# FFN 2's down-projection for token chunks 0 and 1 by Strassen's seven products

## The reference

```python
def swiglu(x, w_in, w_out):
    gate, up = jnp.split(x @ w_in, 2, axis=-1)
    return (jax.nn.silu(gate) * up) @ w_out
...
    y = h + 0.5 * rmsnorm(swiglu(rmsnorm(h, p['ffn2_pre']), p['ffn2_w_in'], p['ffn2_w_out']), p['ffn2_post'])
```

## Time and profile before

| | |
|---|---|
| time, median of 3 runs | 3401.08 us (3397.26 to 3401.41) |
| span of the profiled execution | 3400.1 us, 70872 instructions |
| PE busy | 3305.8 us, 97% of the span |
| DVE busy | 1871.2 us, 55% |
| ACT busy | 1456.3 us, 43% |
| POOL busy | 700.0 us, 21% |
| granted TensorE clock, mean | 0.987 of full speed |
| DMA | 390.03 MB, mean 115 GB/s |

### The profile page before, as it was taken

One profiled execution on the slowest core, in us unless ns is written; L12 is line 12 of the kernel. 1 busy time (PEld: TensorE's weight loads), 2 busy tenths in 40 slices (PEclk: granted clock), 3 DMA queues, 4 the chain that ended last, 5 costly groups with the idle time before them and its releaser, 6 DMA issues. The chain is left out here.

```text
span 3400.1 us, 70872 instructions
## 1 busy us (share of the span) xinstructions
PE 3305.8 (97%) x28190; PEld 3137.6 (92%) x28190; DVE 1871.2 (55%) x3334; ACT 1456.3 (43%) x3056; POOL 700.0 (21%) x651
## 2 busy tenths in 40 slices
...
GB/s 167 76 79 79 87 109 230 221 135 81 70 70 70 71 70 70 109 254 369 188 47 56 58 59 59 59 59 136 165 88 70 123 86 76 76 76 151 200 207 132
DMA packets 353606, 390.03 MB, mean 115 GB/s; under 512 B 22792, under 2 KB 259416, under 8 KB 353134
## 3 DMA queue, kind: packets, MB, share of 16 engines
...
## 5 line engine op out<-in xcount | busy, mean ns | idle before, releaser
L673 PE MATMUL ps<-p_hi,w_hi 128*128 128x352 f32 x912 | 305.6, 335 | 1.8 <-PEq L123 1.4
L673 PE MATMUL ps<-p_hi,w_lo 128*128 128x352 f32 x912 | 294.5, 323 | 0.0
L673 PE MATMUL ps<-p_lo,w_hi 128*128 128x352 f32 x912 | 294.0, 322 | 0.0
L2062 PE MATMUL ps<-p_hi,w_hi 128*128 128x352 f32 x840 | 291.0, 346 | 2.7 <-PEq L123 1.4
L2062 PE MATMUL ps<-p_hi,w_lo 128*128 128x352 f32 x840 | 277.2, 330 | 0.0
L2062 PE MATMUL ps<-p_lo,w_hi 128*128 128x352 f32 x840 | 277.2, 330 | 0.0
L673 PEld LDWEIGHTS ps<-p_hi,w_hi 128*128 128x128 f32 x912 | 173.1, 190 | 4.2 <-issue 2.7
L2897 PE MATMUL ps<-op_hid_hi,w_hi 128*128 128x384 f32 (+1 forms) x528 | 171.5, 325 | 3.7 <-DVE w_lo L2572 2.0
L673 PEld LDWEIGHTS ps<-p_lo,w_hi 128*128 128x128 f32 x912 | 173.2, 190 | 0.0
L2897 PE MATMUL ps<-f_hid_hi,w_hi 128*128 128x352 f32 x528 | 171.5, 325 | 1.6 <-DVE w_lo L2572 1.6
L673 PEld LDWEIGHTS ps<-p_hi,w_lo 128*128 128x128 f32 x912 | 172.2, 189 | 0.0
...
## 6 DMA issues: line engine op xcount, KB each, us to landing
w_raw<-in_ffn_w_out_dram SPq DMA_DIRECT2D x136, 256.0 KB, 3.4
w_raw<-in_w_in_dram SPq DMA_DIRECT2D x67, 512.0 KB, 4.2
sa_v<-in_cache_v_dram SPq DMA_DIRECT2D x120, 256.0 KB, 6.7
w_raw<-in_ffn_w_in_dram SPq DMA_DIRECT2D x48, 512.0 KB, 5.1
sa_k<-in_cache_k_dram SPq DMA_DIRECT2D x72, 256.0 KB, 5.5
f_s<-in_ffn_w_out_dram SPq DMA_DIRECT2D x64, 256.0 KB, 3.5
pair_s<-in_ffn_w_out_dram SPq DMA_DIRECT2D x64, 256.0 KB, 3.2
d_hid<-f_gb SPq DMA_DIRECT2D x44, 264.0 KB, 2.1
```

The lines of the kernel that those rows point to most:

```text
L673: mm = nc.tensor.matmul(m.ps[:, bank, 0:CH], a[:, k, w], b[:, f, cols(c)], start=(f == 0 and i == 0), stop=(f == KT - 1 and i == 2))
L2062: mm = nc.tensor.matmul(m.ps[:, (k + c) % 2, 0:CH], a[:, k, f * P:(f + 1) * P], x[:, f, cols(c)], start=(j == 0), stop=(j == len(terms) - 1))
```

## The change

`ffn_units` gets an argument `quads`, which only FFN 2 passes. For chunks 0 and 1 (768 tokens) the product of 2816 x 1024 weights and 768 tokens is cut in halves along all three axes, and computed with seven products of half the size in each direction instead of eight. A product is now called a pass p (0 to 6); it has KH = 11 units, v = 11 p + k, each again with 4 x 3 matmuls of 384 columns. Chunk 2 keeps the direct product (units 77 to 120, `rest_step`).

- Weights: five passes need the sum or difference of two 128 x 512 tiles, in 55 units in all. SP loads both into the same ring of 8 raw slots (132 loads where there were 88), DVE adds them in place (`w_sum`), and only then ACT and DVE split the sum. Four of the raw slots are freed by `w_low`, the others by `w_sum`.
- Activations: POOL issues accumulating DMAs from DRAM to DRAM during the first half of FFN 2 (`add_stored`, `add_lower`: 11 each into `d_sum`, `d_first` and two parts of `d_hid`); SP stores each of the first 11 tiles twice more as their start (`store_sums`). One operand is made by DVE (`x_sum`, L2723 of the kernel after, 3 pieces). The operand of a pass is loaded whole, a pass ahead, and split in 3 pieces of 4, 4 and 3 tiles (`x_high`, `x_low`, 128 x 1536 or 128 x 1152) instead of 44 pieces of 128 x 384.
- Results: ACT and DVE add each pass's 4 banks to one or two of the four blocks of the output in SBUF during the next pass (`read_act`, `read_dve`), so squares, root, scaling, residual and transposes of chunks 0 and 1 get new places.
- Chunk 2's activations are split by ACT and POOL (`rest_high`, `rest_low`) during pass 6 and after it.

The core of the diff:

```diff
+    SOURCES = (((1, 1),), ((0, 1), (1, 1)), ((0, 0), (1, 0)), ((0, 0), (1, 1)), ((1, 0), (1, 1)), ((0, 0),), ((0, 1), (0, 0)))
...
+    def load_raw(sp, r):
+        v, n = RAWS[r]
...
+        elif RAWS[r - 8][1] == 1:
+            sp.wait_ge(e.w_sum, SUM_OF[RAWS[r - 8][0]])
+        else:
+            sp.wait_ge(e.out_lo, RAWS[r - 8][0] + 1)
...
+    def add_stored(pool, s):
...
+        pool.dma_start(d_first[j], hid_part(s, 0), accum_op=ALU.add).then_inc(e.added[0], 16)
+        pool.wait_ge(e.h_out[1], 16 * (s + 1))
+        pool.dma_start(hid_part(j, 1), hid_part(s, 1), accum_op=ALU.add).then_inc(e.added[5], 16)
...
+    def load_first_parts(sp, g):
...
+        sp.wait_ge(e.added[0], 16 * hi)
+        sp.dma_start(FIRST[g], d_first[lo:hi].rearrange("k p n -> p k n")).then_inc(e.first_in[g], 16)
...
+    def w_sum(dve, v):
...
+        nc.vector.tensor_tensor(unit_raw(r), unit_raw(r), unit_raw(r + 1), ALU.subtract if v // KH in MINUS else ALU.add).then_inc(e.w_sum, 1)
...
+    def w_high(act, v):
+        if v in SUM_OF:
+            act.wait_ge(e.w_sum, SUM_OF[v])
...
+            act.wait_ge(e.out_mm, used(v - 4))
...
+    def quad_scalar(act, during):
+        for v in range(NQ):
+            p, k = divmod(v, KH)
+            w_high(act, v + 3)
+            if p == 0:
+                if k == 5:
+                    x_high(act, 0, 2)
...
+            else:
+                if k == 0:
+                    read_act(act, p - 1)
+                elif p == 1 and k in (2, 5, 7, 9):
+                    x_high(act, 1 if k == 2 else 2, {2: 2, 5: 0, 7: 1, 9: 2}[k])
+                elif k in (2, 4, 6) and 1 < p < 6:
+                    x_high(act, p + 1, k // 2 - 1)
...
+    def quad_vector(dve, during):
+        for v in range(NQ):
+            p, k = divmod(v, KH)
+            w_low(dve, v + 3)
+            if v + 4 in SUM_OF:
+                w_sum(dve, v + 4)
+            if p == 0:
+                if k == 6:
+                    x_low(dve, 0, 2)
+                elif k in (8, 10):
+                    x_low(dve, 1, k // 2 - 4)
+            elif p == 1:
+                if k in (3, 6, 8, 10):
+                    x_low(dve, 1 if k == 3 else 2, {3: 2, 6: 0, 8: 1, 10: 2}[k])
+            else:
+                if k == 0:
+                    read_dve(dve, p - 1, False)
+                elif k == 1 and p == 2:
+                    x_sum(dve, 0)
+                elif k == 2:
+                    if p == 2:
+                        x_sum(dve, 1)
+                    read_dve(dve, p - 1, True)
+                elif k in (3, 5, 7) and p < 6:
+                    x_low(dve, p + 1, (k - 3) // 2)
+                elif k == 4 and p == 2:
+                    x_sum(dve, 2)
...
@@ vector's during, end of chunk 0 and 1
+                pairs = {(5, 9): (0, 0), (5, 10): (0, 1), (6, 1): (0, 2), (6, 3): (0, 3), (7, 10): (1, 0), (7, 11): (1, 1), (7, 12): (1, 2), (7, 13): (1, 3)}
+                sums_of = {(6, 4): (0, 0), (6, 5): (0, 1), (7, 14): (1, 0), (7, 15): (1, 1)}
...
@@ tensor's during
+                if h == 6 and k in (7, 8, 9):
+                    turn(k - 7)
```

More of the change, by code:

```diff
@@ L2368, in ffn_units @@
     e.y_normed, e.h_resid = sem("y_normed"), sem("h_resid")
+    if quads:
+        e.first_in = [sem(f"first_in{g}") for g in range(3)]
+        e.quad_in = {p: sem(f"quad_in{p}") for p in (1, 2, 4, 5, 6)}
+        e.w_sum, e.x_sum, e.x_out = (sem(n) for n in ("w_sum", "x_sum", "x_out"))
+        e.added = {p: sem(f"x_added{p}") for p in (0, 4, 5, 6)}
+        d_first, d_sum = quads
+        e.rest_hi, e.rest_lo = sem("rest_hi"), sem("rest_lo")
+        e.read_act, e.read_dve = sem("read_act"), sem("read_dve")
     win = w_in.rearrange("o (f p) n -> p (o f) n", p=P)
@@ new lines, in quad_there, with x_sum, x_high @@
+    def quad_there(eng, p):
+        eng.wait_ge(e.quad_in[p], 16 * KH)
+    def x_sum(dve, g):
+        lo, hi = GROUPS[g]
+        part = slice(lo, hi)
+        quad_there(dve, 2)
+        dve.wait_ge(e.hid_lo, part_count(1, g))
+        nc.vector.tensor_tensor(HOME[3][:, part, :], HOME[1][:, part, :], HOME[2][:, part, :], ALU.subtract).then_inc(e.x_sum, 1)
+    def x_high(act, p, g):
+        if p == 0:
+            act.wait_ge(e.first_in[g], 16)
+        elif p == 3:
+            act.wait_ge(e.x_sum, g + 1)
+        else:
+            quad_there(act, p)
+        if p == 1:
+            act.wait_ge(e.up_mm, 12 + N1)
+        if p == 0:
+            act.wait_ge(e.up_mm, 12 + N1 - 7 + (2, 3, 4, 6)[(GROUPS[g][1] * W3 - 1) // (HALF * HT)])
+        elif p >= 2:
+            act.wait_ge(e.out_mm, KH * (p - 1))
+        nc.scalar.copy(x_slot(hid_hi, p, g), x_value(p, g)).then_inc(e.hid_hi, 1)
@@ new lines, in lower_rest @@
+    def lower_rest(v):
+        return v >= NQ and (v - NQ) % FT >= KH
+    def w_high(act, v):
+        if v in SUM_OF:
+            act.wait_ge(e.w_sum, SUM_OF[v])
+        else:
+            raw_there(act, RAW_OF[v])
+        if v < 4:
+            act.wait_ge(e.up_mm, 12 + N1 - 10 + v + 1)
+        else:
+            act.wait_ge(e.out_mm, used(v - 4))
+        if lower_rest(v):
+            nc.scalar.mul(unit_slot(v, False), unit_raw(RAW_OF[v]), -1.0).then_inc(e.out_hi, 1)
+        else:
+            nc.scalar.copy(unit_slot(v, False), unit_raw(RAW_OF[v])).then_inc(e.out_hi, 1)
@@ new lines, in add_block @@
+    def add_block(q, i, j, sign=1.0):
+        for half in range(2):
+            y = block_of(i, j, half)
+            if q in (1, 2):
+                nc.vector.wait_ge(e.read_act, READ_ACT[q - 1] + half + 1)
+            if sign > 0:
+                nc.vector.tensor_tensor(y, pass_bank(q, half), y, ALU.add).then_inc(e.read_dve, 1)
+            else:
+                nc.vector.scalar_tensor_tensor(out=y, in0=pass_bank(q, half), scalar=-1.0, in1=y, op0=ALU.mult, op1=ALU.add).then_inc(e.read_dve, 1)
@@ new lines, in read_dve @@
+    def read_dve(dve, q, second):
+        if not second:
+            dve.wait_ge(e.out_mm, KH * (q + 1))
+            wait(dve, e.read_dve, READ_DVE[q - 1])
+        if q == 1:
+            if not second:
+                add_block(q, 1, 0)
+        elif q == 2:
+            if not second:
+                add_block(q, 0, 0)
+        elif q == 3:
+            add_block(q, *((1, 1) if second else (0, 0)))
+        elif q == 4:
+            if not second:
+                add_block(q, 0, 0, -1.0)
+        elif q == 5:
+            add_block(q, *((1, 1) if second else (0, 1)))
+        elif not second:
+            add_block(q, 1, 1)
@@ L2958, in square @@
         c, o = divmod(j, KT)
-        act.wait_ge(e.out_mm, output_done(j))
+        src = result(j)[0]
+        if quads and c < 2:
+            if j == 0:
+                for s in range(2):
+                    act.wait_ge(e.h_out[s], 16 * FT)
+            i = (o + HALF) % KT if c == 0 else o
+            act.wait_ge(e.read_dve, ((10, 2), (12, 16))[c][i // HALF])
+            src = acc[c][:, i, :]
+        elif quads:
+            act.wait_ge(e.out_mm, NQ + 24 * (o // 4) + tail(4 + o // 4) + o % 4 + 1)
+        else:
+            act.wait_ge(e.out_mm, output_done(j))
         if o == 0:
@@ L2965, in square @@
             act.wait_ge(e.y_pooled, 7 * c + o - 4)
-        nc.scalar.activation(ring(c, o) if o else total(c), result(j)[0], ACT.Square).then_inc(e.y_squared, 1)
+        nc.scalar.activation(ring(c, o) if o else total(c), src, ACT.Square).then_inc(e.y_squared, 1)
     def copy_out(dve, j):
```

513 lines of the change are left out of this document (434 added, 79 removed).

## The result

The changed kernel takes 3417.15 us (median of 4 runs, 3410.61 to 3420.73) against 3401.24 us (3397.26 to 3401.93): ratio 1.0048, 95% interval 1.0036 to 1.0060. It is 16 us slower; the forecast was 3403, with a range from 3387 to 3415.

The account below looks back on a forecast made before the run. PE, busy 97% of the span, was taken as the bound, its saving eaten by waits for DVE: 3400.1 - 22.9 - 1.9 + 4.9 + 13.8 + 6.5 + 1.5 = 3402.0 span, median 1.0 above: 3403 us, range 3387 to 3415.

Parts of the forecast that it names:

- third operand piece: Pass 0: the piece lands late, at about 3137, so PE's unit 8 starts late: +4.9 us (3 to 9).
- chunk 2: Chunk 1's root moves right ahead of the residual rows' copies, so the copy for PE's unit 11 is late: +1.5 us.
- sums' chain: Low part, sum, ACT's high part, next low part in sequence: 1.98 us per plain iteration, longer with other DVE work.
- 11 units of PE: Chunks 0 and 1 take 77 units instead of 88, at 2.08 us each: 22.9 us of PE's time go.
- stall at unit 3: At the start, unit 3 began late because of a late low part; it now comes in time: -1.9 us.
- summed units, passes 1 to 4: DVE lags 18.6 us, less 4.84 in hand, so PE waits 13.8 us for low parts.
- transposes in pass 6: PE's first transpose of chunk 0 waits for both residual sums on a late DVE: +6.5 us (3 to 9).
- 4.84 us in hand: Down-projection before the change: DVE ends a low part 1.4 us into unit v; PE needs it at 6.24 us.
- Rival 2: DMAs set the summed units' pace, from a 6.5 us landing on: 3412 or 3424 us; 0.25 with rival 3 and longer waits.
- Rival 3: Accumulation is slow, each us beyond 8 delaying the third piece by 1: 3411 at 16 us; 0.25 with rival 2, longer waits.
- Rival 1: DVE keeps up and its lag stays within 4.84 us: 3387 us; chance 0.32 with mixtures of shorter waits.
- small operation of POOL: Passes 3 and 6: each POOL operation beside DVE's work was taken to cost DVE 0.6 us.

Follow-up runs that it names:

- c: Changed kernel with every weight sum formed over 8 of its 512 columns only: 3403.28 us, against 3400.62 for the kernel before.
- e: Changed kernel with VectorE's sum of unit v+4 put ahead of the low part of unit v+3: 3413.42 us, against 3399.58 for the kernel before.
- f: Changed kernel with GpSimd's last two accumulating DMAs held back until pass 0 has ended: 3421.78 us, against 3399.58 for the kernel before.
- g: Changed kernel with all 44 accumulating DMAs moving 8 of their 128 partitions: 3414.83 us, against 3399.58 for the kernel before.
- m: Changed kernel with chunk 1's residual load in chunk 2 moving one of its eight parts: 3420.11 us, against 3400.07 for the kernel before.
- d: Changed kernel with 52 extra matmuls on PE filling the wait before unit 8 of pass 0: 3417.50 us, against 3400.62 for the kernel before.

## Why the prediction was wrong

The stage was to grow by 1.9 us (3402.0 - 3400.1) and grew by 16.9. Two terms of the sum were far too small, the third operand piece and chunk 2: together 6.4 us were forecast and 20.7 measured. And a slower clock behind PE's long waits, 5.9 us in all, was put at nothing. The sums' chain, which the forecast turned on, was right. By the prediction's own terms:

| term | predicted | measured |
|---|---|---|
| 11 units of PE | -22.9 | -22.9 |
| stall at unit 3 | -1.9 | -1.9, no wait before unit 8 |
| third operand piece | +4.9 | 10.1 wait + 2.1 clock = 12.2 |
| summed units, passes 1 to 4 | +13.8 | lag 30.0 - 4.8 in hand - 12.2 of the start = 13.0 |
| transposes in pass 6 | +6.5 | 6.5 wait + 1.9 clock = 8.4 |
| chunk 2 | +1.5 | 100.1 - 91.6 = 8.5 |

The measured column sums to 17.3; 0.7 us less for a wait of the kernel before in chunk 1 that is gone too leaves 16.6, so 0.3 us are in no term.

- **Right: the chain of a summed unit.** The 1.98 us, the lengthening by an extra, the 4.84 us in hand and the wait in pass 6 are as forecast, and c and e confirm the cause. Its parts partly cancel: lag +4.9, 5.8, 2.1 and 4.9 by the table against 4.4, 4.5, 4.0 and 3.0. That the total comes so near is in part luck. In pass 1, c shows that 4.1 of it is not the sums'.
- **Mis-sized: the third piece (+4.9).** Counted from the first matmul of the stage, the piece was issued 2.6 us later than I had it (14.1 instead of 11.5), and "another 0.6 MB and POOL's three accumulations" were counted as bytes at 360 GB/s; it took 9.0 us from issue to landing, not about 6.3. Together that is 5.3 us, and the wait was 5.2 longer than forecast. f and g show that the two late accumulations alone cost 2.3 us. The upper bound of 9 had come from a landing 21.9 us behind the first matmul (3141); it landed after 23.1, just beyond. The chain behind it was 3.8 us, as worked out (3.7).
- **Mis-sized: chunk 2 (+1.5).** The step named the root of chunk 1 only. It left out that the residual's load and the row stores move from 37 us and more before chunk 2 into its first 12 us, where each unit's weights have 1.6 us. m shows the load as about 3 us of it and 1.9 are the clock; the rest is open.
- **Missing: the clock.** A wait was priced at its own length. PE's matmuls behind the three long waits run at half pace: in pass 0 15 of them at 0.32 instead of 0.173 us, 2.1 us; in pass 6 eight transposes (1.62 instead of 0.79 us) and seven matmuls, 1.9; in chunk 2 eight transposes and nine matmuls of 288 columns, 1.9. It is 5.9 us in all by the rows. With the clock held up, d came out of pass 1 only 0.8 to 1.3 us earlier, so part of the 2.1 would have been lost to the next waits anyway. The profile before showed no such stretch; behind its longest wait there, 1.70 us, the granted clock is 1.00 (3127 to 3132).
- **The rivals.** Rival 2, DMAs setting the pace, holds for the start and, as far as m shows it, for the head of chunk 2, and not for the passes, where `w_raw` and `pair_s` land after a median of 4.2 and 4.4 us, below the 6.5 that I had as the deciding point, and VectorE's sums wait 0.2 us for them. Rival 3, slow accumulation, is refuted by g. Rival 1 is refuted by the lag of 30.0 us at unit 55: VectorE's plain work fits in three of the passes, but the chain takes longer, in part by the order of its calls (e).

Beside that, a small operation of POOL cost more than I took. In pass 3 the sum that meets POOL takes 1.50 us instead of 0.68, 0.82 more, three times, where 0.6 were taken:

```profile
3232.76 1.09 POOL L3495 TENSOR_TENSOR op_gb<-op_gb 128x384 f32<-128x384 f32 x1 [1.71 <-ACT op_gb L3480]
```

```profile
3232.90 1.50 DVE L2748 TENSOR_TENSOR w_raw<-w_raw 128x512 f32<-128x512 f32 x1
```

They overlap from 3232.90 to 3233.85, 0.95 us. The error is not one of those that made the sum too small: pass 3 as a whole added 2.1 us of lag and not 4.0. The Trainium skill (SBUF — State Buffer, "SBUF: two separate sides") has one of the two hold the shared ports for a whole instruction; 0.82 of 0.95 us is nearer to that rule than the "little over half" that I had read from the earlier trace rows.
